# Writing a relative-bias line to memory 128 times and reading it back at a shorter pitch, in place of permutation products on TensorE

## What is computed

```python
def t5_bucket(rel):
    ...
    return jnp.where(rel < exact, rel, jnp.minimum(large, REL_BUCKETS - 1))
...
bias_t = rel_bias.T.reshape(G, R, REL_BUCKETS).astype(f32)
...
logit_c = jnp.einsum('bqgrd,bcgd->bgrqc', qf, kc) + bias_t[:, :, t5_bucket(rel_c)]
...
bias_s = bias_t[gi5, ri5, t5_bucket(rel_s)[:, :, None]]
```

## Time and profile before

| | |
|---|---|
| median of 3 runs | 3007.19 us (3006.07 to 3011.74) |
| the profiled execution, its own time | 3008.65 us |
| its span, first to last instruction | 3006.8 us |
| mean granted TensorE clock | 0.964 of full |
| TensorE busy | 2709.5 us, 90% |
| VectorE / ScalarE / GpSimd busy | 56% / 28% / 22% |
| data moved by DMA | 839.77 MB |

### The profile page before, as it was taken

One profiled execution on the slowest core, in us unless ns is written; L12 is line 12 of the kernel. 1 busy time (PEld: TensorE's weight loads), 2 busy tenths in 40 slices (PEclk: granted clock), 3 DMA queues, 4 the chain that ended last, 5 costly groups with the idle time before them and its releaser, 6 DMA issues.

```text
span 3006.8 us, 31883 instructions
## 1 busy us (share of the span) xinstructions
PE 2709.5 (90%) x12596; PEld 1932.2 (64%) x12596; DVE 1676.1 (56%) x2518; ACT 846.4 (28%) x1241; POOL 675.0 (22%) x647
## 2 busy tenths in 40 slices
PE   8999999999999999999999787887777887778789
PEld 7999899988999888787798333333333333333347
DVE  4454555544455555545567788755554555555455
ACT  4444544443444444335443000000000100000024
POOL 0000000000000000000003655565454464554510
PEclk9999999999999999999999888999999999999999
DMA  7555555556555556552357999999999999999984
GB/s 246 168 161 163 169 184 184 182 193 195 185 184 186 189 194 206 168 165 78 115 172 282 417 422 421 422 422 422 422 422 415 421 422 422 422 422 422 422 323 143
DMA packets 229983, 839.77 MB, mean 279 GB/s; under 512 B 16215, under 2 KB 23731, under 8 KB 163812
## 3 DMA queue, kind: packets, MB, share of 16 engines
q0 software_dynamic: 73728, 536.90, 43.0%
q1 hardware_dynamic: 155084, 298.44, 30.3%
q10 hardware_dynamic: 1048, 2.70, 0.3%
HBM read 835.86 MB, written 2.13 MB: 279 GB/s over the span
## 4 chain that ended last, share of the span: by engine, by line
PE 63%; DMA 21%; DVE 7%; POOL 4%; issue 4%; ACT 2%; ACTq 0%; POOLq 0%; DVEq 0%
DMA vrows<-in_peer_u,idxc 17%; PE bank L2121 9%; PE bank L1674 8%; PE bank L1677 8%; PE bank L1676 8%; PE bank L1696 7%; PE bank L1700 7%; PE bank L1698 7%; DVE vrows L1532 3%; DMA big<-in_peer_u,idxc 3%; POOL idxc L2237 1%; POOL vrows L2246 1%; PE bank L2056 1%; PE bank L2057 1%; PE bank L2058 1%
## 5 line engine op out<-in xcount | busy, mean ns | idle before, releaser
L943 DVE TENSOR_TENSOR wl<-raw,wh 128x1024 fp32r<-128x1024 f32 x544 | 653.3, 1210 | 684.7 <-ACT wh L531 682.3
L531 ACT CAST wh<-raw 128x1024 fp32r<-128x1024 f32 x544 | 560.3, 1038 | 735.1 <-PE bank L1677 364.0
L1696 PE MATMUL bank<-Ah,wh 128*128 128x256 f32 x1792 | 508.4, 284 | 0.6 <-DVE wl L943 0.6
L1700 PE MATMUL bank<-Ah,wl 128*128 128x256 f32 x1792 | 507.1, 283 | 0.0
L1698 PE MATMUL bank<-Al,wh 128*128 128x256 f32 x1792 | 507.1, 283 | 0.0
L1532 DVE CUSTOM_DVE_ANT_0 big<-big,tmp 128x2048 f32<-128x2048 f32 x128 | 288.4, 2290 | 234.4 <-DMA big<-in_peer_u,idxc 234.4
L1532 DVE CUSTOM_DVE_ANT_0 vrows<-vrows,tmp 128x2048 f32<-128x2048 f32 x128 | 288.3, 2290 | 219.4 <-DMA vrows<-in_peer_u,idxc 217.3
L842 ACT ACTIVATE hgel<-hcur,rstd 128x2 f32<-128x2 f32 x128 | 37.7, 295 | 1188.0 <-DVE hcur L1532 1188.0
L1696 PEld LDWEIGHTS bank<-Ah,wh 128*128 128x128 f32 x1792 | 343.9, 192 | 0.9 <-issue 0.8
L1698 PEld LDWEIGHTS bank<-Al,wh 128*128 128x128 f32 x1792 | 344.0, 192 | 0.1
L1700 PEld LDWEIGHTS bank<-Ah,wl 128*128 128x128 f32 x1792 | 343.9, 192 | 0.0
(11 more groups left out here) (312 smaller groups left out, 3750.1 us busy)
## 6 DMA issues: line engine op xcount, KB each, us to landing
raw<-in_mlp_w SPq DMA_DIRECT2D x128, 1024.0 KB, 5.1
raw<-in_sb_w_qkv SPq DMA_DIRECT2D x48, 1024.0 KB, 5.1
raw<-in_w_in SPq DMA_DIRECT2D x28, 1024.0 KB, 5.1
raw<-in_sb_w_o SPq DMA_DIRECT2D x16, 1024.0 KB, 5.1
raw<-in_w_out SPq DMA_DIRECT2D x16, 1024.0 KB, 5.1
raw<-in_peer_w_q SPq DMA_DIRECT2D x16, 1024.0 KB, 5.2
raw<-in_ple_w_gate SPq DMA_DIRECT2D x16, 1024.0 KB, 5.1
tmp<-line SPq DMA_DIRECT2D x4, 768.0 KB, 6.4
```

The costliest lines, as they stand in the source:

```text
L531: nc.scalar.copy(whv[hq % 4][:, :, 0:width], raw_half[hq][:, :, 0:width]).then_inc(hi_done, 1)
L943: V_.tensor_tensor(wlv[hq % 4][:, :, 0:width], raw_half[hq][:, :, 0:width], whf[hq % 4][:, :, 0:width], ALU.subtract).then_inc(split_done, 1)
L1696: nc.tensor.matmul(o, whv[s][:, c, bs_], xh[:, kc, :], start=kc == 0 and b % 2 == 0, stop=False, skip_group_check=True)
L1700: mm = nc.tensor.matmul(o, wlv[s][:, c, bs_], xh[:, kc, :], start=False, stop=kc == KC - 1, skip_group_check=True)
```

## The change

The line is stored to a new memory tensor `lines` of shape (16, 128, 512), so 128 times for each head, 4 MB in one DMA. It is read back starting at place 127 with a pitch of 511 elements: row p of the copy lies 512 p further on, so partition p gets the line from place 127 - p, which is the table the right way up, and it lands in `TB` itself. The store moves from behind job 2 to behind job 1, the four reads stand behind jobs 3, 4, 5 and 6. The products, the copies and their places in the bank order are gone.

```diff
-_uses = [..., ("line", 1), ("flip", 6),
-         ("ct", 2), ("qt", 4), ("flip2", 6), ("gt", 1), ...
+_uses = [..., ("line", 1),
+         ("ct", 2), ("qt", 4), ("gt", 1), ...
...
+        lines = nc.dram_tensor("lines", (16, P, 512), F32, kind="Internal").ap()
...
@@ sync: behind the loads of job n
-                if n == 2:
+                if n == 1:
                     wait_aux_evac(sp, X["line"])
-                    sp.dma_start(line_dram, gbc[0:16, 0:512]).then_inc(line_stored, 16)
-
-                    sp.wait_ge(line_stored, 16)
-                    for n4 in range(2):
-                        sp.dma_start(Xp[n4], bass.AP(line_dram.tensor, n4 * 4 * 512, [[1, P], [512, 4], [1, TRI_W]])
-                                     ).then_inc(xp_landed[n4], 16)
-                if n == 4:
-                    for n4 in range(2, 4):
-                        wait_aux_evac(sp, flip_use(3 * (n4 - 2) + 2))
-                        sp.dma_start(Xp[n4 - 2], ...).then_inc(xp_landed[n4 - 2], 16)
+                    sp.dma_start(lines, gbc[0:16, 0:512].unsqueeze(1).broadcast_to((16, P, 512))).then_inc(line_stored, 16)
+                if n >= 3 and n < 7:
+                    if n == 3:
+                        sp.wait_ge(line_stored, 16)
+                    f0 = 4 * (n - 3)
+                    sp.dma_start(TB[:, f0:f0 + 4, :], bass.AP(lines.tensor, f0 * P * 512 + P - 1,
+                                                              [[511, P], [P * 512, 4], [1, TRI_W]])
+                                 ).then_inc(tb_landed, 16)
...
@@ vector
-            def take_flips(piece):
-                for f in range(3 * piece, 3 * piece + 3):
-                    k = flip_use(f)
-                    dve.wait_ge(aux_done, k + 1)
-                    V_.tensor_copy(big[:, 10240 + f * 512:10240 + f * 512 + 512], aux(k)[:, :]
-                                   ).then_inc(aux_evac[k % 4], 1)
...
-                if n == 2:
-                    take_flips(0)
-                    take_flips(1)
-                if n == 5:
-                    take_flips(2)
-                    take_flips(3)
...
             k = X["csc"]
+            dve.wait_ge(tb_landed, 16 * 4)
             dve.wait_ge(aux_done, k + 1)
...
@@ tensor: flips(0), flips(1) behind job 2 and flips(2), flips(3) behind job 5 are gone
-            def flips(piece):
-
-                pe.wait_ge(xp_landed[piece % 2], 16 * (piece // 2 + 1))
-                for f in range(3):
-                    k = flip_use(3 * piece + f)
-                    wait_aux_free(pe, k)
-                    nc.tensor.matmul(aux(k)[:, :], flip, tmp[:, ...], start=True, stop=True).then_inc(aux_done, 1)
...
@@ gpsimd
-            wait_aux_evac(pool, X["flip2"] + 4)
-            wait_aux_evac(pool, X["flip2"] + 5)
             nc.gpsimd.memset(flat[:, :, :, NCMP:], 0.0).then_inc(pads_ready, 1)
```

More of the change, by code:

```diff
@@ L47 @@
 H_NORM0, H_NORM1, H_NORM2, H_MIX, H_NORM3 = 0, 16, 32, 48, 64
-_uses = [("gain", 1), ("norm0", 8), ("sb", 48), ("norm1", 8), ("norm2", 8), ("line", 1), ("flip", 6),
-         ("ct", 2), ("qt", 4), ("flip2", 6), ("gt", 1), ("kt", 2), ("hid", 2), ("mixed", 2), ("cmp", 1),
+_uses = [("gain", 1), ("norm0", 8), ("sb", 48), ("norm1", 8), ("norm2", 8), ("line", 1),
+         ("ct", 2), ("qt", 4), ("gt", 1), ("kt", 2), ("hid", 2), ("mixed", 2), ("cmp", 1),
          ("mixed2", 2), ("kct", 1), ("csc", 1), ("pool", 4), ("pct", 2), ("norm3", 8), ("skt", 4), ("psc", 8)]
@@ L71, in win_width @@
     return WIN_REST if WIN_BLOCKS[n] == 7 else 512
-def flip_use(f):
-    return X["flip"] + f if f < 6 else X["flip2"] + f - 6
 def mixed_use(u):
@@ L236, in build @@
         Pc3 = v3(big, 1024, 8, P)
-        Xp = [v3(tmp, n * 1536, 4, TRI_W) for n in range(2)]
         sA = [v3(tmp, n * 512, 2, S) for n in range(4)]
@@ L315, in build @@
         line_stored = sem("line_stored")
-        xp_landed = [sem("xp_landed0"), sem("xp_landed1")]
+        tb_landed = sem("tb_landed")
         sk_landed = sem("sk_landed")
@@ L434, in _ @@
                     sp.dma_start(gbc[0:33, 512:1024], a["onehot"]).then_inc(oh_landed, 16)
-                if n == 2:
+                if n == 1:
                     wait_aux_evac(sp, X["line"])
-                    sp.dma_start(line_dram, gbc[0:16, 0:512]).then_inc(line_stored, 16)
-                    sp.wait_ge(line_stored, 16)
-                    for n4 in range(2):
-                        sp.dma_start(Xp[n4], bass.AP(line_dram.tensor, n4 * 4 * 512, [[1, P], [512, 4], [1, TRI_W]])
-                                     ).then_inc(xp_landed[n4], 16)
-                if n == 4:
-                    for n4 in range(2, 4):
-                        wait_aux_evac(sp, flip_use(3 * (n4 - 2) + 2))
-                        sp.dma_start(Xp[n4 - 2], bass.AP(line_dram.tensor, n4 * 4 * 512, [[1, P], [512, 4], [1, TRI_W]])
-                                     ).then_inc(xp_landed[n4 - 2], 16)
+                    sp.dma_start(lines, gbc[0:16, 0:512].unsqueeze(1).broadcast_to((16, P, 512))).then_inc(line_stored, 16)
[6 more added lines that the diff above has]
+                                 ).then_inc(tb_landed, 16)
             for q in range(4):
@@ L1813, in _ @@
                         rows_job(j2 + 2 * n + kq, a2 + n, x=H_, k0=16 * kq, first=kq == 0, last=kq == 1, before=before)
-            def flips(piece):
-                pe.wait_ge(xp_landed[piece % 2], 16 * (piece // 2 + 1))
-                for f in range(3):
-                    k = flip_use(3 * piece + f)
-                    wait_aux_free(pe, k)
-                    nc.tensor.matmul(aux(k)[:, :], flip, tmp[:, (piece % 2) * 1536 + f * 512:(piece % 2) * 1536 + f * 512 + 512],
-                                     start=True, stop=True).then_inc(aux_done, 1)
             def gate_job(j, n):
@@ L1883, in _ @@
                                      ).then_inc(aux_done, 1)
[L1884 to L1889, removed]
             pe.wait_ge(pads_ready, 1)
```

## The result

The changed kernel takes **3030.64 us** (median of 6 runs, 3027.77 to 3034.03), the kernel before 3009.37 in runs on the same chips. The ratio is 1.0073, with a 95% interval of 1.006 to 1.0085: slower by 0.7%, 21.3 us.

The account below looks back on a forecast made before the run. It took TensorE to bound the stage, and the new store in SP's queue to decide. Products removed -11.6, stall +27.3 and lower clock +4 gave +19.7 us: 3027 us against the median, range 3004 to 3066.

Parts of the forecast that it names:

- The likeliest case: At job 2, its first load waits behind the slow 16-partition store and TensorE stalls; 3027 us, chance 0.62.
- Products removed: TensorE behind jobs 2 and 5: 5.65 and 6.3 us won, 0.4 lost to a late split; together -11.6 us.
- The reads back: Four 768 KB reads behind jobs 3 to 6: pitch 511 and their new places cost nothing.
- The store's data: SP's queue behind job 1: 4.19 MB from 16 partitions at 110 GB/s takes T = 38 us.
- The proportional rival: Store behind job 1: rate falls in full proportion to partitions, 55 GB/s, T = 76 us, 3065 us; chance 0.12.
- The slack: Job 2's first load: TensorE stalls for the store's data time T less 10.7 us, so +27.3 us.
- The lower clock: TensorE after the stall at job 2: some ten us of products at half clock, +4 us.
- The sum: Whole kernel: -11.6 + 27.3 + 4 = +19.7 us, giving 3027 us against the median.
- The range: Whole kernel: 3004 to 3066 us, leaving out the rival at 2996 and taking in those at 3008 and 3065.
- The full rate: Store behind job 1: runs at 400 GB/s or loads overtake it, no stall, 2996 us; chance 0.19.
- The rate of the 64 partitions: Store behind job 1: 221 GB/s, T = 19 us, stall 8.3 us, 3008 us; chance 0.07.
- What would show it right: One TensorE stall of 20 to 35 us at job 2, store at 90 to 125 GB/s, gaps at jobs 3 and 6 gone.

Follow-up runs that it names:

- one_copy: The changed kernel with its store writing one copy of the line (32 KB), read at pitch 1, so the table lands upside down; 2998.88 us.
- half: The changed kernel with 64 copies (2 MB) stored from the same 16 partitions, read at pitch 253, so the table is wrong; 3011.95 us in one run.
- wide32: The changed kernel with the line made on 32 partitions, each storing 64 copies, the same 4 MB; 3010.20 us in one run.
- wide64: The changed kernel with the line made on 64 partitions, each storing 32 copies, the same 4 MB; 3006.95 us in one run.
- spread16: The changed kernel with the line made on 128 partitions and the 4 MB stored from 16 of them, eight apart; 3011.84 us in one run.
- parts4: The changed kernel with its 16-partition store in four 1 MB pieces behind jobs 1 to 4, reads behind jobs 6 and 7; 2997.15 us.

## Why the prediction was right

The time was forecast at 3027 us, slower by 0.65%; it is 3030.64, slower by 0.7%. The likeliest case is the one that came, for its reason: the store's data holds job 2's first load. The loss was forecast at 19.7 us and is 21.3, and the other 2 us of the gap are mostly the median of the kernel before, which stands at 3009.37 and not 3007.19. Term by term:

- *Products removed*, -11.6: the one_copy run has -11.4 at the mark and -10.3 in the medians. The 0.4 us of a late split at job 6 is in the trace as 0.42.
- *The reads back*, nothing: in the changed kernel the last of them leaves at 1289.25 and lands 9.7 us later, and VectorE takes the table at 1367.59, after a wait for TensorE:

```profile
1367.59 1.37 DVE L1240 TENSOR_TENSOR big<-bank,big 128x60 f32<-128x60 f32 x8 [7.20 <-PE bank L1913]
```

- *The store's data*, T = 38 us from a rate of 110 GB/s between two bounds: the rate was 102, T = 41. To take the middle of 55 and 221 was a choice and not a reading, and that it came this near was luck as much as judgement. The reason given with it, that the rate follows how many partitions a transfer touches, is not what the runs show: 32 and 64 partitions do the same 210 GB/s, and 16 that lie apart do 197. The rows of before could not tell that half the partitions halve the rate for another reason than their number. The proportional rival was off by a factor of two at 16.
- *The slack*, T - 10.7: the stall is 31.1 for a T of 41.0, so the slack is 9.9; half shows 10.7, with 9.9 of stall for 20.5 of data, and wide32, wide64 and spread16, with T of 20 to 21, show 9.1 to 9.6. The load was converted from 1212.56, where the reading gave 1171.1 + 41.0 = 1212.1.
- *The lower clock*, +4: 2.2 us, eleven steps and not some twenty. In the stretch that I took, of granted clock 0.83, TensorE was busy for only 15.81 of 20 us, so part of the low clock there lay over waits; how long it stays low after this stall no row of before could tell.
- *The sum* at the mark: -11.4 + 31.1 + 2.2 = 21.9, measured 21.7. The forecast had the stall 3.8 us too small and the clock 1.8 too large, and these partly cancel.
- *The range.* The rivals at 2996, 3008 and 3065 fell. The full rate was seen only from 128 partitions. The rate of the 64 partitions is real too, from 32 on. That the loads might overtake the store was refuted in SP's queue, and in a queue of their own they only share.
- *What would show it right* was seen: one wait of TensorE, at job 2, the engines busy at about 100 GB/s, the gaps at jobs 3 and 6 gone. ScalarE's wait was 38.2 us, where T less 5 gives 36, and the low clock lasted 4.7 us, not 10.

## What to carry to other kernels

In this kernel a store cost its bytes over the rate that its SBUF partitions allow (102 GB/s from 16 neighbours, some 210 from 32 or 64, 382 from 128), and it was charged to whatever stood behind it in its queue and, in part, to loads in another queue. So before a small tile is multiplied in memory, spread its source over all 128 partitions. The large transfer in a queue of timely loads cost nothing up to the slack of the next load and full price beyond; pieces below that slack, with room for the loads to catch up, cost nothing that could be measured. Products that TensorE saves are worth their full time only where everything that they covered is early, so read the slack of what comes next before counting them.

## What the runs showed that I had not expected

Behind the mark the profiled executions differ by more than the experiments explain. From the compression's last scores (the 32 small products) on, the same work takes different times. In the kernel before, and then in the changed one:

```profile
1338.74 5.27 PE L1948 MATMUL bank<-big 128*128 128x32 f32 x32 [2.40 <-DVE big L1250]
1343.82 8.98 PE L1957 MATMUL bank<-gbc,mrows 128*128 128x256 f32 x32
```

```profile
1360.44 7.04 PE L1913 MATMUL bank<-big 128*128 128x32 f32 x32 [2.40 <-DVE big L1229]
1367.29 10.05 PE L1922 MATMUL bank<-gbc,mrows 128*128 128x256 f32 x32
```

The wait ahead is 2.40 us in both, but the granted clock is 0.70 over the small products in the one, and 0.50, the lower of the two levels (1.2 and 2.4 GHz), in the other:

```profile
1338.70:1343.80 5.10, 5.06 (x32) 5.06 (x33) 0.00 (x0) 0.00 (x0) 0.00 (x0) 0.70 0.90 332
```

```profile
1360.40:1367.30 6.90, 6.86 (x33) 6.86 (x33) 0.00 (x0) 0.00 (x0) 0.00 (x0) 0.50 0.67 247
```

What differs is when the clock falls. In the kernel before it is still 1.00 over the wait and 0.94 over the first 2.3 us of the small products; in the changed one it has fallen within the wait, over which it is 0.82. That is 2.8 us of the 25.3 by which the two spans differ, and it is not the change's: half, which has the change's order too, took 5.25 and 9.00 us there, as the kernel before did, and parts4, without any stall of TensorE at jobs 2 to 5, took 7.04 and 8.51. Over thirteen profiled executions the time from the scores to the products of `big` and `tmp`, the third group behind them, is 16.5 (four times) to 19.3 us, and from the mark to the end it is 1689 to 1697 us. Why the clock falls sooner in some executions was not found, and where the rest of those 8 us lies was not looked for. Differences of two or three us between single runs of this kernel can be of this kind, which is why the mark was used.
